# An expert layer that interleaves the small pieces of a 32-row tail with full weight pieces: where TensorE does the tail pieces and the tail's turns

## The reference, cut to what matters

```python
logits = (xt @ w_router + b_router).astype(jnp.float32)
top_val, top_idx = lax.top_k(logits, TOP_K)          # 4 of 32 experts
...
def expert_rows(args):                                # one group of rows, one expert
    rows, e = args
    gu = rows @ w_gate_up[e] + b_gate_up[e]
    gate = jnp.minimum(gu[:, :D_FF], SWIGLU_LIMIT)
    up = jnp.clip(gu[:, D_FF:], -SWIGLU_LIMIT, SWIGLU_LIMIT)
    hid = (up + 1.0) * (gate * jax.nn.sigmoid(gate * SWIGLU_ALPHA))
    return hid @ w_down[e] + b_down[e]
```

## Time and profile before

| | us |
|---|---|
| median of 3 runs | 2486.85 (2484.39 to 2487.14) |
| the profiled execution, its own time | 2487.02 |
| its span | 2485.4 |
| TensorE busy in it | 2351.9 (95%) |
| VectorE busy | 1809.3 (73%) |
| ScalarE busy | 1405.0 (57%) |
| share of the chain of waits that is TensorE's | 74% |

### The profile page before, as it was taken

How to read it: one execution, slowest core, us unless ns; L and a number is a source line. 1 busy time by engine, 2 the same in 40 slices (tenths; PEclk the granted TensorE clock), 3 DMA queues, 4 the chain that set the end, 5 groups by cost and what they waited for, 6 DMA issues and landing times.

```text
span 2485.4 us, 39291 instructions
## 1 busy us (share of the span) xinstructions
PE 2351.9 (95%) x11242; PEld 1565.7 (63%) x11243; DVE 1809.3 (73%) x2101; ACT 1405.0 (57%) x1441; POOL 251.4 (10%) x252
## 2 busy tenths in 40 slices
PE   6999999999949999999999999999999999999898
PEld 3454455545536777677777776777676676776443
DVE  4583565545466989788998997899787787897374
ACT  2113344444435777677777776677665675776344
POOL 1200000002130000100000001000111010010230
PEclk9999999999959999999999999999999999999999
DMA  6006910052337999989999999899988898997661
GB/s 196 21 14 218 356 30 23 13 196 70 111 107 269 326 369 348 324 306 373 347 361 365 347 365 344 295 349 357 344 287 283 270 361 277 364 350 262 264 220 51
DMA packets 291341, 629.55 MB, mean 253 GB/s; under 512 B 21633, under 2 KB 69505, under 8 KB 291218
## 3 DMA queue, kind: packets, MB, share of 16 engines
q1 hardware_dynamic: 235538, 532.20, 61.1%
q10 hardware_dynamic: 40304, 55.05, 6.1%
q0 software_dynamic: 15440, 41.51, 5.2%
HBM read 558.55 MB, written 68.57 MB: 252 GB/s over the span
## 4 chain that ended last, share of the span: by engine, by line
PE 74%; DVE 11%; DMA 6%; issue 5%; ACT 2%; DVEq 1%; SPq 1%; POOL 0%; ACTq 0%; POOLq 0%
PE bank L610 14%; PE bank L612 12%; PE bank L611 12%; PE bank L1363 6%; DVE wlo L871 5%; PE bank L775 4%; PE bank L1476 4%; PE bank L1386 3%; DMA raw<-in_w_down_dram 3%; PE bank L671 3%; PE bank L1353 2%; PE bank L1406 2%; PE bank L580 2%; PE bank L1435 2%; DVE sig L891 1%
## 5 line engine op out<-in xcount | busy, mean ns | idle before, releaser
L871 DVE TENSOR_TENSOR wlo<-raw,whi 128x2048 fp32r<-128x2048 f32 x456 | 1038.0, 2286 | 206.0 <-PE bank L612 160.5
L1748 ACT ACTIVATE whi<-raw 128x2048 fp32r<-128x2048 f32 x456 | 872.2, 1914 | 357.2 <-PE bank L612 186.1
L610 PE MATMUL bank<-whi,xhi 128*128 128x512 f32 x1216 | 502.9, 414 | 11.1 <-issue 10.9
L612 PE MATMUL bank<-wlo,xhi 128*128 128x512 f32 x1216 | 482.1, 396 | 0.0
L611 PE MATMUL bank<-whi,xlo 128*128 128x512 f32 x1216 | 481.9, 396 | 0.0
L610 PEld LDWEIGHTS bank<-whi,xhi 128*128 128x128 f32 x1216 | 229.7, 189 | 109.3 <-issue 60.3
L612 PEld LDWEIGHTS bank<-wlo,xhi 128*128 128x128 f32 x1216 | 229.4, 189 | 55.4
L611 PEld LDWEIGHTS bank<-whi,xlo 128*128 128x128 f32 x1216 | 229.8, 189 | 45.5
L610 PE MATMUL bank<-whi,hhi 128*128 128x512 f32 x608 | 246.9, 406 | 0.0
L611 PE MATMUL bank<-whi,hlo 128*128 128x512 f32 x608 | 237.4, 390 | 0.0
L612 PE MATMUL bank<-wlo,hhi 128*128 128x512 f32 x608 | 237.4, 390 | 0.0
(11 more groups left out here) (294 smaller groups left out, 2758.4 us busy)
## 6 DMA issues: line engine op xcount, KB each, us to landing
raw<-in_w_gate_up_dram SPq DMA_DIRECT2D x608, 512.0 KB, 6.1
raw<-in_w_down_dram SPq DMA_DIRECT2D x152, 1024.0 KB, 10.3
expert_rows<-zeros ACTq DMA_DIRECT2D x1, 33280.0 KB, 105.1
expert_rows<-ysb ACTq DMA_DIRECT2D x38, 512.0 KB
xall<-in_x_dram SPq DMA_DIRECT2D x8, 512.0 KB, 13.2
uT<-in_w_out_dram SPq DMA_DIRECT2D x1, 4096.0 KB, 13.2
raw<-in_w_ple_gate_dram SPq DMA_DIRECT2D x1, 4096.0 KB, 20.1
h<-h_scratch SPq DMA_DIRECT2D x8, 512.0 KB, 9.3
```

Source lines behind the costliest of these rows:

```text
L610: pe.matmul(dst, stat_hi[:, kt], hi, start=first, stop=False)
L612: return pe.matmul(dst, stat_hi[:, kt], lo, start=False, stop=last)
L871: dve.tensor_tensor(wlo[:, c % LO], raw[:, c % RAW], whi[:, c % HI].bitcast(F32), ALU.subtract).then_inc(lo_ready, 1)
L1748: act.activation(whi[:, c % HI], raw[:, c % RAW], ACT.Copy).then_inc(hi_ready, 1)
```

## The change

TensorE: tail pieces come two by two. Behind main pieces 1, 3, 5, 7 of a tail item stand tail pieces (4,5), (6,7), (8,9), (10,11), and behind main pieces 9 and 11 of the item before stand (0,1) and (2,3) of the next tail. The turn of the tail's second inner half and the turn of the next tail's rows move into main piece 6, right behind the first main turn. ScalarE: the copy of the tail's second inner half comes after the copy of the main half.

```diff
-            def gate_piece(n, c):
+            def gate_piece(n, c, turns):
...
                     if c == 6 and g == 1:
-                        turn_hidden(n, 0)
+                        turns()
...
             def body(n, k1, tail):
                 nk1 = k1 + tail
+                def turns():
+                    turn_hidden(n, 0)
+                    if tail:
+                        turn_tail_hidden(k1, 1)
+                        pe.wait_ge(sums_ready, 2 * k1 + 2)
+                    with pe.If(nxt2 > 0):
+                        turn_tail_rows(n + 1, items.kf + tail)
...
                     if tail and c == 1:
                         turn_tail_hidden(k1, 0)
-                    if tail and c + AHEAD < PIECES:
+                    if tail and c in (1, 3, 5, 7):
+                        tail_piece(n, k1, c + AHEAD - 1)
                         tail_piece(n, k1, c + AHEAD)
-                    if tail and c == 5:
-                        turn_tail_hidden(k1, 1)
...
-                    if c == 6:
-                        if tail:
-                            pe.wait_ge(sums_ready, 2 * k1 + 2)
-                        with pe.If(nxt2 > 0):
-                            turn_tail_rows(n + 1, items.kf + tail)
...
-                    if c + AHEAD >= PIECES:
+                    if c in (9, 11):
                         with pe.If(nxt2 > 0):
+                            tail_piece(n + 1, nk1, c + AHEAD - PIECES - 1)
                             tail_piece(n + 1, nk1, c + AHEAD - PIECES)
...
                 for c in range(PIECES):                    # ScalarE
-                    if tail and c in (2, 6):
-                        tail_hidden(k1, c // 4)
+                    if tail and c == 2:
+                        tail_hidden(k1, 0)
...
                     if c in (6, 8):
                         hidden(n, c // 8)
+                    if tail and c == 6:
+                        tail_hidden(k1, 1)
```

More of the change, by code:

```diff
@@ L701, in body @@
                 nk1 = k1 + tail
+                def turns():
[5 more added lines that the diff above has]
+                        turn_tail_rows(n + 1, items.kf + tail)
                 for c in range(PIECES):
                     pe.wait_ge(lo_ready, PIECES * n + c + 1)
-                    mm = gate_piece(n, c) if c < 8 else down_piece(n, c)
+                    mm = gate_piece(n, c, turns) if c < 8 else down_piece(n, c)
                     mm.then_inc(w_free, 1)
```

## The result

The changed kernel takes 2471.66 us (median of 4 runs, 2470.31 to 2474.51) beside 2486.99 us for the kernel before (4 runs, 2484.39 to 2489.06) on the same chip: a ratio of 0.9943, with a 95% interval of 0.9929 to 0.9957. That is 15.3 us less. The profiled execution took 2471.6 us at a granted clock of 0.979 (before: 0.981).

The account below looks back on a forecast made before the run. TensorE, busy 95% of the span, was taken to bound the kernel. Seven usual tails at 1.98 us (13.9), plus 0.7 for the first, minus 0.2, made 14.4 us: 2487.02 to 2472.6 us, range 2467.0 to 2481.0.

Parts of the forecast that it names:

- part 1: Tail pieces on TensorE: two side by side cost 2.05 us instead of 2.40; 0.34 us less taken for each of 46 pairs.
- Rival (b): The second piece of a pair costs the full 1.00 us, its own wait coming first: 2479.5 us; chance 0.06.
- rival (d): Tail matmul groups don't overlap, so a second piece costs 1.52 us instead of 0.85: 2503.4 us; chance 0.01.
- part 2: Register read for the next item, now right behind main piece 4: 0.68 us less for each of eight tails.
- part 3: First tail turn comes too early: new 0.60 us wait on `hid_t`, 0.15 for following waits; this pair loses 0.40 us.
- the first tail item: Three pairs gain 1.02 us, the pair behind its first tail turn loses 1.00, the register read gains 0.68: 0.7 gained.
- part 4: Second tail turn and turn of next tail's rows, moved behind the first main turn: counted nothing, 0.2 us more for a double tail.
- rival (a): The branch in the middle of main piece 6 shows, 0.25 us in each of 30 items: 2480.1 us; chance 0.12.
- part 5: Load queues: slots come free up to 4 us later, but loads may start 6 us later before ScalarE waits: nothing.
- The sum: A usual tail gains 1.98 us, seven 13.9; the first gains 0.7; minus 0.2 for the double tail: 14.4 us.
- items without a tail changed their length: Sign that the prediction is wrong: items without a tail should keep their length, with 0.36 us behind the first main turn.

Follow-up runs that it names:

- the pair taken apart: The changed kernel with the next tail's pieces 0 and 1 split behind main pieces 8 and 9, one branch test put back: 2473.95 us, ratio 0.995.
- the version without the wait: The changed kernel with the first tail turn moved from behind main piece 1 into the middle of main piece 2: 2459.26 us; repeated, 2461.5 us.
- The experiments with fours: Changed kernel with first tail turn in main piece 2, plus blocks of four: throughout, 2473.84 us; with pieces 8 to 11 paired, 2461.29; one block only, 2463.08.
- the turns put back: The changed kernel with both moved turns back behind tail piece 9 and main piece 6, pairs kept: 2473.49 us, ratio 0.9947.
- its two moved copies: The kernel before with two or eight long-satisfied waits added on TensorE ahead of the expert loop: 2492.52 us with two, 2482.08 with eight.

## Why the prediction was right

**The price of a pair (part 1)** was taken as 0.34 us and is 0.36, by the pair taken apart. The second piece costs 0.86 where 0.85 was read from the earlier trace rows. Rival (b), with 1.00, and rival (d), with 1.52, are excluded: the weights of the next four matmuls are loaded while the four ahead, with the same rows, still run, in pairs and in fours (in the single piece of the earlier trace rows too, where the 16 weight loads lie within 0.59 us and the matmuls take 1.07). The rule of the Trainium skill beside (d) (TensorE: Matmul & The Clock Gate, Part 3, The mechanism), that weight loads overlap running matmuls only in another row group, doesn't hold for these pieces.

**The table read (part 2)** was taken as 0.68 and is 0.78. It was the second largest term, and right by its mechanism: read first, with nothing else changed, the gap goes.

**The new wait (part 3)** was taken as 0.60 us and 0.15 for what follows it. The 0.60 is right to the hundredth by starts: without a wait the turn would stand 0.24 us behind the last main matmul, at 1546.97, and it stands at 1547.57. The trace puts 0.44 of that down as idle time. The 0.15 was too much: the step from the turn to the pair is 0.24, where it was 0.20 ahead of a single piece. Together 0.64, and the version without the wait is 0.67 shorter. In the first tail item 1.75 us and what one piece less brings, some 2.95, were expected, and 2.93 measured. Without the wait the parts close: six pairs at 0.36 and the read at 0.78 make 2.94 us, and 52.33 - 49.40 = 2.93.

**The moved turns (part 4)** were counted at nothing. Two experiments, one with the turns alone and one without them, say the same. The step behind the first main turn in items without a tail is 0.35 us (before 0.36), with the test of the branch now in it:

```profile
1173.83 0.60 PE L597 MATMUL bank<-cst,hid 128*128 128x128 f32 x4
1174.18 0.48 PE L610 MATMUL bank<-whi,xhi 128*128 128x512 f32 x1
```

So rival (a) is excluded: `hid` is early enough to cover the test. In a tail item the tail turn stands behind the main turn, and the step is 0.46 us:

```profile
1567.10 0.60 PE L597 MATMUL bank<-cst,hid 128*128 128x128 f32 x4
...
1567.54 0.27 PE L687 MATMUL bank<-cst,hid_t 128*128 128x128 f32 x1
1567.56 0.48 PE L610 MATMUL bank<-whi,xhi 128*128 128x512 f32 x1
```

So it adds 0.11 us there, where it had cost 0.09 behind a tail piece.

**The loads (part 5)** were given 6 us to spare, and in the changed kernel no load held up TensorE: ScalarE's waits for gate and up loads grew from 53.6 to 68.3 us in all, but no matmul waits for a low part in the stage. The experiments with fours show how near the edge that was: loads that start 5.4 us later in an item made ScalarE wait 5.58 us there and TensorE 2.00. The 6 us to spare were read in one item, and are fewer where tail items follow one another.

**The sum.** A usual tail was to gain 1.98 us and gains 2.26: 0.12 from pairs (six at 0.02), 0.10 from the read and 0.08 from the wait, which is the difference but for 0.02. Seven of them are 15.8 us instead of 13.9, if the last tail item, which lies behind the last turn of rows, gains what the six measured ones do.

**The first tail item is what it had wrong.** It was to gain 0.7 us, and it lost. Four executions have pairs with the turn behind main piece 1 (the changed kernel twice, the turns put back, the pair taken apart): their first interval is 56.12 to 57.28 us. Five have single pieces (the kernel before, its two moved copies, the read first, the turns only): 54.96 to 55.91. The means differ by 1.3 us, the wrong way. The step that failed is the loss of 1.00 us behind the turn of this item. Its wait was right, but the pair behind the wait was priced at the higher clock, and it ran at 1.2 GHz: from the turn to the next main matmul are 3.58 us (754.23 - 750.65), where 1.24 + 0.85 + 0.15 = 2.24 were reckoned. All four executions wait 2.93 or 2.94 us there and show a granted clock of 0.50 behind the turn, and the next pair comes 1.4 to 2.8 us later than in a usual tail item. The five with single pieces wait 0.72 to 1.89 us there and keep 1.00, and so do the two with the turn in main piece 2, which don't wait at all. The prediction reckoned with the higher clock level throughout the stage.

**Luck.** The seven tails brought 1.9 us more than was reckoned and the first one about 2.0 less, and these cancel. That the forecast lies within 0.9 us of the median is owed to that. That each term of a usual tail item came within about 0.1 us is not luck.

The prediction also says that it would be wrong if items without a tail changed their length. They did, by 0.15 us in the usual one, while the mechanism held. It took the code's place on the engine as without effect, and it reckoned from one execution, where executions of one kernel differ by 5 us ahead of the stage and by 4 in its first items.

## What to carry to other kernels

Where an engine switches between two kinds of work, the price of a block is a fixed part for the switch and a part per piece; read both from blocks of different length that the trace already has, and multiply. Before work is moved away from a place, look at what waited behind its cover: here each block taken away exposed a wait on `hid_t` or `hid`, and moving the waiting turn half a main piece later brought 10 to 12 us more, beside the 15 of the change. A wait can also cost more than its length: look at the granted clock behind it, as the first tail item shows. And before a difference of 0.1% is put down to an edit, move the code by a few instructions that do nothing and see whether that alone gives it.

## What was not expected of the hardware

- TensorE's clock fell to 1.2 GHz (granted 0.50) at the end of a single wait of 2.93 us in the middle of busy work, in all four executions that had it, and was back after 3 to 7 us; the work behind the wait cost 1.4 to 2.8 us more. In the ten others, with waits of 0 to 1.89 us at the first tail turn, it stayed at 2.4 GHz (granted 1.00).
- The place of the loop's code on TensorE changes an item by up to 0.26 us (38.26 us moved by two instructions, 38.15 as it was, 38.00 moved by eight), with the work and its order the same. It shows at the turn of rows, as a longer group or as a gap of 0.19 us ended by "issue".
- A read of two registers behind a tail piece costs 0.78 us where 32 queued instructions are all that covers it, and shows no gap where a main piece of 2.8 us does.
- Blocks of 128x32 weight loads and 256-column matmuls cost 0.86 us a piece at the full clock for the second piece, and on average for the second to the fourth, and a block fewer saves 0.31 to 0.36 us.
